# Grouping the last units of a projection by token tile, and turning the next stage's first tile inside the group

## The reference

```
for layer in (0, 1):                                # sandwich norms
    y = rms_norm(h, nw[0]);  y = even_mixer(y) or odd_mixer(y)
    h = h + rms_norm(y, nw[1])
    y = conv_ffn(rms_norm(h, nw[2]))                # 1024 -> 2 x 2816 -> 1024
    h = h + rms_norm(y, nw[3])
h = second_block(h)                                 # three attentions with gates, merged @ w_out, then a SiLU feed-forward
```

## Time and profile before

| | us |
|---|---|
| median of 3 runs | 1212.09 |
| lowest, highest | 1208.49, 1223.79 |
| span of the profiled execution | 1223.9 |
| TensorE busy | 1159.9 |
| VectorE busy | 703.4 |
| ScalarE busy | 543.4 |
| GpSimd busy | 82.5 |

### The profile page before, as it was taken

The page is one execution under the profiler, slowest core; times in us unless marked ns, Lnnn a source line. Parts: engine busy times, 40 slices in busy tenths (PEclk is TensorE's granted clock), DMA queues, the critical chain, the costliest instruction groups (busy, mean ns, idle before and its releaser), DMA issues.

```text
span 1223.9 us, 18229 instructions
## 1 busy us (share of the span) xinstructions
PE 1159.9 (95%) x7292; PEld 1041.4 (85%) x7292; DVE 703.4 (57%) x938; ACT 543.4 (44%) x756; POOL 82.5 (7%) x113
## 2 busy tenths in 40 slices
PE   5999997999998999997999997999999998999998
PEld 4898676999987786877999986888999997999986
DVE  5668435666654536446666645576555684555553
ACT  5345324545543346324554534435644633444441
POOL 3300002000001001001000002013000000000000
PEclk9998577999999899587999998999999998999999
DMA  6854013545555354024555553554322353555552
GB/s 258 307 186 138 1 53 128 199 171 181 195 177 202 138 195 165 19 89 152 177 190 183 176 202 137 184 181 169 138 104 104 120 191 111 196 174 176 194 182 100
DMA packets 28875, 194.15 MB, mean 159 GB/s; under 512 B 3488, under 2 KB 3680, under 8 KB 6800
## 3 DMA queue, kind: packets, MB, share of 16 engines
q1 hardware_dynamic: 25760, 183.58, 42.1%
q0 software_dynamic: 3056, 9.73, 2.4%
HBM read 192.25 MB, written 1.05 MB: 158 GB/s over the span
## 4 chain that ended last, share of the span: by engine, by line
PE 88%; DVE 5%; ACT 3%; DMA 1%; POOL 1%; issue 1%; SPq 0%; DVEq 0%; ACTq 0%
PE ps L860 41%; PE ps L802 32%; PE ps L920 3%; PE ps L943 2%; PE ps L1057 2%; PE ps L932 2%; PE ps L1075 2%; PE ps L871 2%; DMA raw<-in_weights 1%; DVE lo L1179 1%; DVE xhat L1210 1%; POOL ms L432 1%; PE ps L887 1%; ACT hi L504 1%; PE ps L988 1%
## 5 line engine op out<-in xcount | busy, mean ns | idle before, releaser
L1179 DVE TENSOR_TENSOR lo<-raw,hi 128x2048 fp32r<-128x2048 f32 (+2 forms) x169 | 382.0, 2266 | 174.2 <-ACT hi L504 174.1
L860 PE MATMUL ps<-y_hi,hi 128*128 128x256 f32 x1376 | 393.9, 286 | 3.5 <-DVE y_lo L1230 1.9
L860 PE MATMUL ps<-y_lo,hi 128*128 128x256 f32 x1376 | 392.3, 285 | 0.0
L860 PE MATMUL ps<-y_hi,lo 128*128 128x256 f32 x1376 | 392.2, 285 | 0.0
L504 ACT ACTIVATE hi<-raw 128x2048 fp32r<-128x2048 f32 (+2 forms) x168 | 315.9, 1887 | 147.9 <-DMA raw<-in_weights 141.9
L860 PEld LDWEIGHTS ps<-y_hi,hi 128*128 128x128 f32 x1376 | 267.2, 194 | 5.4 <-issue 3.4
L860 PEld LDWEIGHTS ps<-y_lo,hi 128*128 128x128 f32 x1376 | 267.1, 194 | 0.0
L860 PEld LDWEIGHTS ps<-y_hi,lo 128*128 128x128 f32 x1376 | 267.0, 194 | 0.0
L802 PE MATMUL ps<-hi,h_hi 128*128 128x512 f32 x328 | 102.8, 395 | 3.6 <-DVE h_lo L1230 2.6
L802 PE MATMUL ps<-hi,y_hi 128*128 128x512 f32 (+1 forms) x320 | 101.3, 398 | 3.1 <-DVE y_lo L1230 2.2
L802 PE MATMUL ps<-hi,h_lo 128*128 128x512 f32 x328 | 102.7, 394 | 0.0
(11 more groups left out here) (258 smaller groups left out, 1102.8 us busy)
## 6 DMA issues: line engine op xcount, KB each, us to landing
raw<-in_weights SPq DMA_DIRECT2D x172, 1024.0 KB, 4.8
gain<-in_gains POOLq DMA_DIRECT2D x11, 512.0 KB, 4.9
bias<-in_rel POOLq DMA_DIRECT2D x16, 128.0 KB, 2.8
k<-in_mem SPq DMA_DIRECT2D x2, 512.0 KB, 7.5
h<-in_x SPq DMA_DIRECT2D x1, 1024.0 KB, 15.3
out<-h SPq DMA_DIRECT2D x2, 512.0 KB, 2.6
pick<-in_c_pick POOLq DMA_DIRECT2D x1, 512.0 KB, 7.7
head_gain<-in_head_gains POOLq DMA_DIRECT2D x1, 256.0 KB, 7.4
```

What stands on the lines that cost most here:

```text
L860: mm = pe.matmul(dst, w[:, s % RAW, at], x(k), start=first and k == 0, stop=final and k == nk - 1)
L1179: dve.tensor_tensor(lo[:, s, :w], raw[:, s, :w], hi[:, s, :w].bitcast(F32), ALU.subtract).then_inc(lo_done, 1)
```

## The change

The diff does four things.

- **Tail groups.** The pair at the end of a projection becomes `by_tile`, a group of `TAIL_GROUP` units: all four of even_out, odd_out and merge_out, the last three of the down projections. All their parts of tile 0 come first, then all of tile 1.
- **The turn inside the group.** Ahead of the last part of tile 1, TensorE turns tile 0 of the next stage (`turn_next`), for all but down2. `enter` and `feed_forward` then turn only tile 1.
- **Entries.** `enter` leads with three units by tile instead of two (mem_kv: two, as before). In a group of four that is also an entry, tile 1 is turned ahead of the third unit. The waits on lower halves are split by k.
- **Orders of ScalarE and VectorE.** Tile 0's work is done whole, its turned copies included, before tile 1's product is weighed or squared. Rounding and splits of the next units move behind it: in feature-major stages the split of the first unit stands between the weighing of tile 1's product and its residual add; in token-major stages it stands before that weighing, and the second unit's between the weighing and the add. In the first attention, the last two units of even_out are rounded ahead of the second head's exponentials and split ahead of the third head's maximum.

```diff
 
 TAILS = ["even_out", "down0", "odd_out", "down1", "merge_out", "down2"]
+TAIL_GROUP = {"even_out": 4, "down0": 3, "odd_out": 4, "down1": 3, "merge_out": 4, "down2": 3}
 
 
 def norm_count(g, t):
...
 
 
+                square_product(g, 0, base, tile_done, TAILS.index(name) + 1)
+                square_sum(g + 1, 0, p)
                 units(last(name) + 1)
-                square_product(g, 0, base, tile_done, TAILS.index(name) + 1)
-                units(last(name) + 2)
-                square_sum(g + 1, 0, p)
+                turned_hi(stage, turn_base, y_hi, (0,))
                 square_product(g, 1, base, unit_used, last(name))
-                turned_hi(stage, turn_base, y_hi, (0,))
+                if stage not in FEATURE_MAJOR:
+                    units(last(name) + 2)
                 square_sum(g + 1, 1, p)
+                if stage not in FEATURE_MAJOR:
+                    units(last(name) + 3)
                 turned_hi(stage, turn_base, y_hi, (1,))
+                units(max(last(name) + 2, done[0]))
 
             def head_square(i, src, nh, d):
                 if i >= 2:
@@ -659,6 +664,7 @@
             for t in range(NT):
                 act.wait_ge(mk_turned, t + 1)
                 act.activation(mk_t[:, :, t * P:(t + 1) * P], split4(bank(6 + t)), ACT.Copy).then_inc(mk_evac, 1)
+            units(last("even_out"))
             for hh in range(1, 8):
                 exps("a", hh)
             act.wait_ge(maxed, 8)
@@ -780,8 +786,9 @@
             units(last("merge_out"))
             square_sum(10, 0, 4)
             units(last("merge_out") + 1)
...
-            def tokens_by(name, base, y, splits=((0, 512), (512, 512)), entry=None, ready=None, before_last=lambda: None, needs=None):
+            def tokens_by(name, base, y, splits=((0, 512), (512, 512)), entry=None, stage=None, before_last=lambda: None, needs=None,
+                          turn_next=lambda: None):
 
 
 
@@ -814,23 +822,34 @@
                 def part(n, t):
                     return tokens_unit(name, n, first_k[n - n0], t, base, y, splits)
 
-                def pair(n, between=lambda: None, halfway=lambda mm: None):
-                    wait_unit(n)
-                    part(n, 0)
-                    between()
-                    wait_unit(n + 1)
-                    halfway(part(n + 1, 0))
-                    for m in (n, n + 1):
-                        if ready is not None and m == n0:
-                            pe.wait_ge(*ready)
-                        part(m, 1).then_inc(unit_used, 1)
+                def by_tile(first, count, is_tail):
+
+                    leads = stage is not None and first == n0
+                    for n in range(first, first + count):
+                        wait_unit(n)
+                        if needs is not None:
+                            pe.wait_ge(*needs(n - n0))
+                        if leads and first_k[n - n0] == 4:
+                            pe.wait_ge(y_lo_done, 4 * stage + 2)
+                        if leads and n == first + max(count - 2, 1):
+                            entry(1)
+                        mm = part(n, 0)
+                    if is_tail:
+                        mm.then_inc(tile_done, 1)
+                    for n in range(first, first + count):
+                        if leads and first_k[n - n0] in (0, 4):
+                            pe.wait_ge(y_lo_done, 4 * stage + 3 + first_k[n - n0] // 4)
+                        if is_tail and n == first + count - 1:
+                            turn_next()
+                        part(n, 1).then_inc(unit_used, 1)
 
                 n = n0
-                if entry is not None:
-                    pair(n, lambda: entry(1))
-                    n += 2
-                    pe.wait_ge(ready[0], ready[1] + 1)
-                tail = n1 - 2 if name in TAILS else n1
+                tail = n1 - TAIL_GROUP[name] if name in TAILS else n1
+                if stage is not None and n < tail:
+                    lead = 2 if name == "mem_kv" else 3
+                    by_tile(n, lead, False)
+                    n += lead
+                    pe.wait_ge(y_lo_done, 4 * stage + 4)
                 while n < tail:
                     if n == n1 - 1:
                         before_last()
@@ -841,9 +860,7 @@
                     part(n, 1).then_inc(unit_used, 1)
                     n += 1
                 if name in TAILS:
-                    if needs is not None:
-                        pe.wait_ge(*needs(n + 1 - n0))
-                    pair(n, halfway=lambda mm: mm.then_inc(tile_done, 1))
+                    by_tile(n, TAIL_GROUP[name], True)
 
...
-            def enter(stage, base, name, out_base, ready=normed, counts=None, y=None, before_last=lambda: None):
+            def enter(stage, base, name, out_base, ready=normed, counts=None, y=None, turned_first=False, **more):
 
                 counts = counts or [2 * NORM_OF_TURN[stage] + 1, 2 * NORM_OF_TURN[stage] + 2]
-                turn(stage, xhat, base, 0, ready, counts[0])
+                if not turned_first:
+                    turn(stage, xhat, base, 0, ready, counts[0])
                 pe.wait_ge(y_lo_done, 4 * stage + 1)
-                tokens_by(name, out_base, y or Y, entry=lambda t: turn(stage, xhat, base, t, ready, counts[1]),
-                          ready=(y_lo_done, 4 * stage + 3), before_last=before_last)
+                tokens_by(name, out_base, y or Y, entry=lambda t: turn(stage, xhat, base, t, ready, counts[1]), stage=stage, **more)
+
+            def turn_normed(stage, base, t):
+                turn(stage, xhat, base, t, normed, 2 * NORM_OF_TURN[stage] + t + 1)
...
             pe.wait_ge(mk_evac, 2)
-            enter(2, 4, "even_out", 0, attended, [2, 2])
-
-            def feed_forward(layer, stage, base):
+            enter(2, 4, "even_out", 0, attended, [2, 2], turn_next=lambda: turn_normed(3, 4, 0))
+
+            def feed_forward(layer, stage, base, turn_next=lambda: None):
 
                 up = FIRST[f"up{layer}"]
 
-                for t in range(NT):
-                    turn(stage, xhat, base, t, normed, 2 * NORM_OF_TURN[stage] + t + 1)
+                turn_normed(stage, base, 1)
...
                 each_tile(pe, tile)
-                tokens_by(f"down{layer}", 4, (h_hi, h_lo), needs=lambda u: (h_lo_done, KF * layer + 2 * u + 2))
-
-            feed_forward(0, 3, 4)
-
-            enter(4, 0, "odd_q", 4)
+                tokens_by(f"down{layer}", 4, (h_hi, h_lo), needs=lambda u: (h_lo_done, KF * layer + 2 * u + 2),
+                          turn_next=turn_next)
+
+            feed_forward(0, 3, 4, lambda: turn_normed(4, 0, 0))
+
+            enter(4, 0, "odd_q", 4, turned_first=True)
...
-            enter(5, 0, "odd_out", 4, attended, [3, 4])
-            feed_forward(1, 6, 4)
-
-            enter(7, 0, "moba_qk", 4)
+            enter(5, 0, "odd_out", 4, attended, [3, 4], turn_next=lambda: turn_normed(6, 4, 0))
+            feed_forward(1, 6, 4, lambda: turn_normed(7, 0, 0))
+
+            enter(7, 0, "moba_qk", 4, turned_first=True)
...
-            tokens_by("merge_out", 4, (h_hi, h_lo), needs=lambda u: (merged_lo, u // 2 + 1))
+            tokens_by("merge_out", 4, (h_hi, h_lo), needs=lambda u: (merged_lo, u // 2 + 1),
+                      turn_next=lambda: turn_normed(8, 4, 0))
...
-            def norms_between(g, p, base, name, stage, turn_base, r):
+            def norms_between(g, p, base, name, stage, turn_base):
                 dve.wait_ge(turned, 4 * stage)
                 weigh_product(g, 0, base, tile_done, TAILS.index(name) + 1)
-                units(last(name) + 1)
                 add_product(g, p, 0)
                 weigh(g + 1, 0, [h[:, 0, 0:512], h[:, 0, 512:D]])
-                weigh_product(g, 1, base, unit_used, last(name))
                 scale(g + 1, 0)
+                turned_lo(stage, turn_base, y_lo, y_hi, (0,))
                 if stage in FEATURE_MAJOR:
+                    weigh_product(g, 1, base, unit_used, last(name))
+                    units(last(name) + 1)
                     add_product(g, p, 1)
                     weigh(g + 1, 1, [h[:, 1, 0:512], h[:, 1, 512:D]])
-                    turned_lo(stage, turn_base, y_lo, y_hi, (0,))
                     scale(g + 1, 1)
                     turned_lo(stage, turn_base, y_lo, y_hi, (1,))
                     units(last(name) + 2)
                 else:
-                    turned_lo(stage, turn_base, y_lo, y_hi, (0,))
+                    units(last(name) + 1)
+                    weigh_product(g, 1, base, unit_used, last(name))
                     units(last(name) + 2)
                     add_product(g, p, 1)
-                    norm(g + 1, r, 1, h)
+                    weigh(g + 1, 1, [h[:, 1, 0:512], h[:, 1, 512:D]])
+                    scale(g + 1, 1)
+                    units(last(name) + 3)
                     turned_lo(stage, turn_base, y_lo, y_hi, (1,))
...
@@ -1470,6 +1494,7 @@
```

(9 more changed lines are left out.)

11 lines of the change are left out of this document (6 added, 5 removed).

## The result

The changed kernel took **1234.53 us** (median of four runs, 1232.13 to 1235.12), the kernel before beside it 1217.94 us (four runs, 1208.49 to 1224.26). The ratio is **1.0127, interval [1.0065, 1.0189]**: 1.3% slower, within 2%. A later set of six runs gave 1234.44 and 1.0136 [1.0075, 1.0197]. The profiled execution has a span of 1233.3 us against 1223.9: +9.4.

What follows compares the result with a forecast made beforehand. TensorE, busy 95% of the span, was taken as the bound, so only its pauses, added work and clock count. Terms 3.9 + 0.7 + 1.9 + 1.7 + 1.9 + 2.3 = 12.4 us, added to median 1212.09, gave 1224.5; range 1207 to 1238.

Steps and rivals of the forecast that it cites:

- The 7 us of that bound: Upper bound on unseen stall and clock terms inside tails: turn + 0.9 and a part + 1.95 in three places.
- the rival on the attention's clock: First or second attention: a shifted entry tips the granted clock either way by 12 us, 1212 or 1236; chance 0.15, half each.
- the text's own signs of being wrong: Pauses before tile 1's turn under 7 us, or an attention stage no longer than before.
- Attention, +3.9: First attention before even_out: moved rounding and splits delay the probabilities' copy and first mix, never caught up; +3.9 us.
- even_out, +0.7: even_out to up0: tile 1's chain stays exposed; shorter queueing is eaten by the GpSimd lock and the turn; +0.7 us.
- down0 and down1, +1.9 each: down0 to odd_q, down1 to moba_qk: residual add queued behind splits, +0.9; half-clock restart after longer pause, +1.0; each +1.9 us.
- odd_out, +1.7: odd_out to up1: even_out's 0.7 again plus 1.0 waiting for unit 3's split; +1.7 us.
- merge_out, +2.3: merge_out to up2: waits of 1.7 and 0.5 for splits, then tile 1's exposed chain; +2.3 us.
- the places that I put at nothing: Entries led by three units and down2: claimed to cost nothing.
- The waits go and do not return: Boundaries: tile 1's chain shortens so one pause per boundary disappears; -9, 1203 us; chance 0.15.
- The clock falls inside the tails: Tails: stalls of 1.5 to 1.7 us drop TensorE's clock; +7, 1231 us; chance 0.15.
- It does nothing: Whole kernel: the change has no effect; dismissed because TensorE's own program writes out the parts' order; no chance given.

Runs made afterwards that it cites:

- the filled pair: The kernel before and the changed kernel, each with six extra identity turns ahead of head 9's scores in the second attention: 1209.09 and 1219.85 us.
- e1: Changed kernel, but even_out's last two units are rounded and split in quarters, two a head, behind the first attention's exponentials and copies: 1231.68 us.
- e3: Changed kernel, but after down0 and down1 the second unit's split follows tile 1's second scaling, and tile 1 turns before that unit's wait: 1232.56 us.
- e11: Changed kernel with six extra identity turns ahead of head 9's scores in the second attention: 1219.85 us, ratio 1.001 to the kernel before.
- e10: Kernel before the change with six extra identity turns ahead of head 9's scores in the second attention: 1209.09 us, ratio 0.9947.
- e2: Changed kernel, but at three feed-forward boundaries the next unit's split is queued behind tile 1's second scaling: 1229.59 us, ratio 1.0052 to the kernel before.
- e5: Changed kernel with merge_out's tail group cut from four units to the pair of before: 1234.43 us.
- e9: Changed kernel measured once more, nothing edited: 1234.44 us, six runs.
- e4: Changed kernel, but at the three feed-forward boundaries tile 0 is turned after the tail's last part, as before: 1225.72 us, ratio 1.0069.
- e6: Changed kernel with e1, e3, e4's turn and e5 together, plus the first unit's split halved so none stands beside a root: 1215.05 us, ratio 0.9974.

## Why the prediction was right, and where it was not

The sum was 12.4 us; the two profiles differ by 9.4 and the filled pair by 10.8. Slower by about 1% and within 2% was right, and 1234.5 lies in the range of 1207 to 1238. It lies outside the forecast's own range, 1217 to 1231, and the wide range holds it only because its upper end was set for falling clocks. (The 7 us of that bound is also short: 0.9 + 1.95 in three places is 8.6.) That the sum comes near is in part luck: the six places that it priced came to 9.2 us together (4.0 + 0.1 - 0.7 + 3.0 - 0.3 + 3.1), with errors of either sign. The point, 1224.5, was 10 us low, for a reason that the text itself named: it added the sum to a median of three runs, of which two had the attention's full clock (1208.49 and 1212.09), while the changed kernel never had it. The time of the rival on the attention's clock, 1236, and the sum on the profiled execution, 1236, are both near the 1234.5. So it was this rival's slow half, given a chance of 0.075, that came true beside the forecast's mechanism; ten runs of ten went that way. Whether the shift of the stage tipped the clock, as the rival had it, no run shows.

One of the text's own signs of being wrong appeared as well. It named pauses before tile 1's turn of under 7 us; they are 8.76 and 8.75 at up0 and up1, but 6.50 at both token-major boundaries and 6.17 at up2. At up2 the sign did not fit the sum, which comes to 5.5 us there. At the token-major boundaries it points at the step that failed.

- **Attention, +3.9: right.** +3.85 (e1 took it away in full); the copy followed the splits as said. +0.14 more up to even_out.
- **even_out, +0.7: mechanism right, size by a ramp.** From E0 it is 23.0 against 23.3 put, and before 22.6: +0.4. The turn without a pause (1.03 us), the pause of 8 to 9 us and the long GpSimd operation (2.27 us in tile 1's root, 0.30 in tile 0's) all came as put. The stage as a whole gained the 0.4 back, to +0.1, by a ramp of 3.4 us at its start instead of 4.3; half of that difference is time won.
- **down0 and down1, +1.9 each: the step that failed.** The stages measured -0.7 and -0.3, the boundaries alone, from E0 on, -0.2 and -0.1; the rest is the ramp at the start of up0 and up1. The stall inside the tail (1.40) came as put, the pause (6.50 against 7) nearly so. The residual add was put at E0 + 18.0 and came at 402.61, E0 + 17.0: the queue of splits ahead of it was a microsecond shorter, since tile 1's weighing came at E1 = E0 + 11.5 and not at 12.1. And the second term, 1.0 for a restart from a longer pause, isn't there: the turn took 1.94 us and the half clock behind it ended with the second matmul pair.

```profile
408.42 1.20 PE L809 MATMUL ps<-hi,y_hi 128*128 128x512 f32 x2
409.42 0.87 PE L809 MATMUL ps<-lo,y_hi 128*128 128x512 f32 x2
410.13 0.62 PE L809 MATMUL ps<-hi,y_lo 128*128 128x512 f32 x2
```

  Before, behind a pause of 2.17 us, the turn took 1.67: three times the pause cost 0.3 us more of it. Turn and part together took 5.1 us against 5.3 before and 6.4 put. I had priced the longer pause by the start of odd_out, a row from another place. With e3's order 3.0 us of turn are to be had, as the account by queues said.
- **odd_out, +1.7: right but for a ramp.** The wait for unit 3's split was 1.02 against 1.0 put. The stage took +3.0: 0.46 from E0 to the start against 0.7, and some 1.1 us from a longer ramp at its very start (the tile's turn came 8.33 us in, 535.24 - 526.91; by 7.2 before). I cannot tell this ramp's cause: the work ahead of it is the same. Where the ramps are equal the term stands by itself: e1, with the changed kernel's code here and a ramp of 3.5 us as before, took 38.2 us against 36.3, and e11 36.6 against e10's 34.7, both with 0.6. That is +1.9 each time.
- **merge_out, +2.3: low.** The waits were 1.50 and 0.31 against 1.7 and 0.5. The stage took +3.1. Most of the rest is the root: GpSimd's operation took 2.68 us beside the split (2.17 in the earlier trace rows), and the root was done at 1035.70, 5.55 us after tile 1's add began (1030.15), against 4.9 put.
- **Left out: the places that I put at nothing.** At the turn of the third attention's heads the clock fell behind a pause that before had too. TensorE, and then the stretch with its granted clock of 0.71:

```profile
852.40 2.45 PE L907 MATMUL ps<-ident,qkm 128*128 128x128 f32 x16 [1.98 <-ACT qc L735]
```

```profile
852.00:856.00 4.00, 3.60 (x23) 3.63 (x24) 3.12 (x7) 3.96 (x6) 0.00 (x0) 0.71 0.58 236
```

  Before, the same turns took 1.94 us behind 1.97 us of pause, at clock 1.00. That is +1.6, and it is no price of the change. e1, with the changed kernel's instructions there, had the turns of before:

```profile
851.54 1.94 PE L915 MATMUL ps<-ident,qkm 128*128 128x128 f32 x16 [1.97 <-ACT qc L743]
```

  So had e2 and e3; their stretch to merge_out is 150.7 us, as before, while e5, e9 and e11 have the 152.2. It is a second place whose clock has two levels. The first stretch gave -2.6, and three profiles of the kernel before, e10 among them, spread as much there: 114.1, 111.4 and 110.6 us, against 111.5, 111.5 and 112.6 for the changed one. The last stretch gave +0.8, by a ramp of 5.9 us instead of 4.0 at the start of up2. Its pause ahead was 6.17 us instead of 1.81, but e5 had the same 6.17 and a ramp of 3.5.
- **The rivals.** *The waits go and do not return*: refuted. They went in number, from ten to seven, and returned in length, 30.2 to 39.5. E1 to the second turn is 8.72 us, just above the 8.5 from which it would have decided; with the split away (e2) it is 6.8, and the boundary is 1.3 shorter, so the rival would have needed an order of VectorE that the change did not bring. *The clock falls inside the tails*: refuted, the turns there took 1.03 to 1.10 us, and pauses of 1.1 to 1.5 us left the clock full. *It does nothing*: refuted by the order of the parts.

## What to carry to other kernels

Two short waits that overlap in part aren't won by letting one of them go: what stays is the last chain from TensorE's end to its next start, and only what shortens that chain counts: here a split beside a root (2 us of the pause, 1.3 to 1.5 of the start), a turn inside running work (0.9 us) and splits queued ahead of an add (3 us of the turn, 1.0 of the stage). Before two medians are compared, look for a stage whose clock has two levels in the same kernel: here it was 13 us, more than the change, and with 0.8 us of spare work in the pause ahead of it all 36 runs were at the upper level.

## What the runs showed of the hardware that I had not expected

- Behind a pause of 0.85 us in thin work the granted clock fell from full to half or didn't, in the same program: 68.7 or 81.9 us for the stage. By their times, the kernel before had it full in 35 of 84 runs, the changed one in none of ten, e2 in 3 of 8, e4 in 4 of 8, e6 in none of twelve. With six spare turns (0.82 us) that cut the pause to 0.19 it was full in 6 + 6 + 12 + 12 runs. What decided it in a run without them stays open.
- The same pause of 1.97 to 1.98 us, ahead of the same turns, left the clock at 1.00 in one profile and at 0.71 in the other.
- The stretch at half clock at the start of a projection varies for the same instructions ahead of it: at even_out 3.4 us in two profiles of the changed kernel and 5.2 in e11, which is that kernel up to there; 6.1 in e1. e1 lost 1.3 us of its gain to it, e3 about 1.0 at each of two boundaries.
- GpSimd's operation on 128 x 1 took 0.30 us alone (0.56 to 0.58 where it overlapped the 1.3 us weighing), and 2.17 to 2.68 us beside a 2.28 us split.
